# The 512-column weight-stationary product in every stage of a fused encoder layer, with its evictions, gelu and first LayerNorm reordered

## The chip, the cores and the metric

One core of a Trainium2 chip runs the whole layer as one program. The metric is device microseconds of that core, lower is better. Besides the timed runs there is one execution under the hardware profiler, from which all rows of this document are taken.

## The reference

One post-norm layer over 256 tokens of width 2048, all in float32 (cut):

```python
proj = x @ w_in                       # q, k, v (8 heads x 128), u (1024), two gates (2048 each)
g_att, g_ssm = sigmoid(g_att + b), sigmoid(g_ssm + b)
y_att = neighbourhood_attention(q, k, v, rpb) @ w_na_out
y_s = s5_scan(u, forward) + s5_scan(u, backward) + s5_d * u     # 64 groups, 64 complex states
y_s = gelu(y_s); y_s = y_s * sigmoid(y_s @ w_glu + b_glu)
mix = (g_att * y_att + g_ssm * (y_s @ w_s5_out)) @ w_out
h = layer_norm(ALPHA * x + mix)
out = layer_norm(ALPHA * h + (silu(h @ w_ffn_gate) * (h @ w_ffn_up)) @ w_ffn_down)
```

## The kernel before

All weights come as one stream of 464 pieces of 128 x 1024 numbers, in the order in which they are used: 16 for u (pieces 0 to 15, "the U stage"), 16 for v, 12 for each of the 8 heads (q, k and the two gates, two pieces for each of six outputs), 8 + 8 + 8 for the first half of the attention projection (NA1), the GLU and the second half (NA2), 16 for the S5 output (S5O), 32 for the output projection (WO), 176 for gate and up of the feed-forward stage (FF) and 88 for down (DN).

Each piece goes through the same steps. SP's queue loads it into one of 4 raw buffers (`load`). ScalarE rounds it into a high part (`split_hi`, L510), VectorE subtracts to get the low part (`split_lo`, L885); there are 3 buffers for each, so ScalarE may split piece c once TensorE has used piece c-3. TensorE then multiplies high by high, high by low and low by high. The activations are split in the same way: `act16[:, k, 0, :]` is the high part of 256 tokens, `act16[:, k, 1, :]` the low one, side by side. A piece holds 8 weight tiles of 128 x 128.

There are three forms of the product. `prod_a` (L1375) keeps the weight tile in TensorE and issues three matmuls of 256 columns into one half of a bank; u, the heads and the four mixer projections use it. `prod_w` (L1388), used by FF alone, issues one matmul of 512 columns (high weights by both parts, into both halves of the bank) and one of 256; the two halves are added when the bank is emptied. `prod_b` (L1402) keeps the activations in TensorE and streams 512 weight columns; v, WO and DN use it.

What every engine does besides is written out by hand as a list of small steps between the pieces: `if j == 5: ...` behind piece j of head f. Each engine works its own list in order, and semaphores tie them. The steps that matter here:

In a head, TensorE does `turn_b` (four transposes of the next head's S5 matrices; TURN_B says behind which pieces), `s5_in`, `scores`, `s5_out`, `transposes`, `blocks` and `attend`. ScalarE empties the banks (`loop_copy` L663), keeps the turned matrices (`keep_wb` L576, four times), forms exp and the normalised weights. VectorE runs the scans (`scan`, `turn_back`), the softmax maximum, `form_c` (L1022) for the next head and `finish`. POOL computes tables and `form_b` (L438) for the next head. The lag products are stored to memory and loaded again as tb by ScalarE's queue (`stage_tb` L595).

At the end of the heads ScalarE does `loop_copy(HEADS - 1, 5)` and then its list for NA1: the splits, sigmoids of the gates, and behind the fourth split one gelu over all of u and the high part of it. `na_gate` (L1178), `glu_act` and `s5o_evac` (L1218) multiply straight out of the banks.

The banks of WO are (3 + n - N_WO) % 8 (L243). Behind WO VectorE splits three FF pieces, adds the residual (`residual` L1237), takes the moments and normalises h (L1288). TensorE transposes h in 8 groups; ScalarE applies gain and bias to each from the bank (L818) and rounds it (L821), VectorE forms the low part (L889). When all 8 are transposed, POOL multiplies h by the gain and adds the bias in place, in four operations of 2048 columns (L490, L492); the second LayerNorm needs that.

## Time and profile before

| | us |
|---|---|
| timed runs | 1478.47, 1487.91, 1488.67 |
| median | 1487.91 |
| profiled execution | 1480.08 |
| its span, first to last instruction | 1478.3 |

A timeline row has the start in us from the start of the span, the duration, engine, line, operation, what it writes and reads, a count, and in brackets the idle time of the engine ahead of it with what ended it. A matmul's duration is longer than its share of a stream, since matmuls overlap; the pace is the distance between starts. PE is TensorE, PEld its weight loads, DVE VectorE, ACT ScalarE, POOL GpSimd.

### The profile page before, as it was taken

The numbers are of one execution on the slowest core, as the hardware profiler recorded it, in microseconds if no ns is written. First come the engines' busy times: TensorE is split into PE (matmuls) and PEld (weight loads), VectorE is DVE, ScalarE is ACT, GpSimd is POOL, SyncE is SP. The second block draws the span as 40 slices with busy tenths as digits, with TensorE's granted clock in tenths as the row PEclk, the third lists the DMA queues.
The fourth block names the chain that finished last, engine by engine and source line by source line (L and its number), as shares of the span: only waits on it lengthen the run. The fifth ranks groups of instructions, "written<-read, shape, count | busy, mean of one in ns | idle before, by whom it ended". The sixth has DMA issues, their size and how long they took to land.

```text
span 1478.3 us, 25543 instructions
## 1 busy us (share of the span) xinstructions
PE 1406.1 (95%) x10144; PEld 1266.9 (86%) x10144; DVE 931.0 (63%) x1119; ACT 711.2 (48%) x984; POOL 206.0 (14%) x170
## 2 busy tenths in 40 slices
PE   7899999999999899999599999999999999999994
PEld 7789999999999899888488888888888888888883
DVE  7869777887766456665865555555555554545545
ACT  4354555555553664434455445445445444334342
POOL 2784223442310000000500000000000000000002
PEclk9999999999999999999799999999999999999997
DMA  8564545454445467556155555555755555555662
GB/s 286 165 210 159 174 147 169 151 161 153 158 149 166 130 200 274 169 185 200 54 185 186 196 187 186 194 187 185 250 190 185 192 191 192 192 194 192 196 191 80
DMA packets 87700, 266.53 MB, mean 180 GB/s; under 512 B 13760, under 2 KB 22080, under 8 KB 87104
## 3 DMA queue, kind: packets, MB, share of 16 engines
q1 hardware_dynamic: 79472, 259.86, 53.3%
q10 hardware_dynamic: 8144, 5.48, 1.3%
q8 instruction: 62, 1.02, 0.3%
q14 instruction: 22, 0.18, 0.0%
HBM read 260.19 MB, written 5.11 MB: 179 GB/s over the span
## 4 chain that ended last, share of the span: by engine, by line
PE 91%; DVE 6%; ACT 1%; issue 1%; DMA 0%; ACTq 0%; SPq 0%; DVEq 0%
PE bank L1397 22%; PE bank L1398 11%; PE bank L1383 9%; PE bank L1385 9%; PE bank L1384 9%; PE bank L1410 8%; PE bank L1411 8%; PE bank L1412 8%; PE bank L1471 2%; DVE wlo L885 2%; PE bank L1440 1%; DVE act L889 1%; PE bank L1492 1%; PE bank L1518 1%; PE bank L1453 1%
## 5 line engine op out<-in xcount | busy, mean ns | idle before, releaser
L885 DVE TENSOR_TENSOR wlo<-raw,whi 128x1024 fp32r<-128x1024 f32 x464 | 585.9, 1266 | 436.0 <-ACT whi L510 432.9
L510 ACT ACTIVATE whi<-raw 128x1024 fp32r<-128x1024 f32 x464 | 489.7, 1057 | 438.0 <-PE bank L1412 223.0
L1397 PE MATMUL bank<-act,whi 128*128 128x512 f32 x1408 | 491.2, 395 | 10.8 <-DVE wlo L885 10.8
L1398 PE MATMUL bank<-act,wlo 128*128 128x256 f32 x1408 | 391.2, 278 | 0.0
L1397 PEld LDWEIGHTS bank<-act,whi 128*128 128x128 f32 x1408 | 265.1, 188 | 73.0 <-issue 9.9
L1383 PE MATMUL bank<-act,whi 128*128 128x256 f32 x896 | 261.9, 292 | 10.1 <-DVE wlo L885 10.0
L1398 PEld LDWEIGHTS bank<-act,wlo 128*128 128x128 f32 x1408 | 265.6, 189 | 0.0
L1384 PE MATMUL bank<-act,whi 128*128 128x256 f32 x896 | 254.7, 284 | 0.0
L1385 PE MATMUL bank<-act,wlo 128*128 128x256 f32 x896 | 254.6, 284 | 0.0
L1383 PEld LDWEIGHTS bank<-act,whi 128*128 128x128 f32 x896 | 173.0, 193 | 11.3 <-DVE wlo L885 10.7
L1384 PEld LDWEIGHTS bank<-act,whi 128*128 128x128 f32 x896 | 173.0, 193 | 0.5
L1385 PEld LDWEIGHTS bank<-act,wlo 128*128 128x128 f32 x896 | 172.8, 193 | 0.0
L1412 PE MATMUL bank<-whi,mid 128*128 128x512 f32 x352 | 137.0, 389 | 0.0
L1410 PE MATMUL bank<-whi,mid 128*128 128x512 f32 x352 | 137.0, 389 | 0.0
L1411 PE MATMUL bank<-wlo,mid 128*128 128x512 f32 x352 | 137.0, 389 | 0.0
L498 POOL TENSOR_TENSOR hp<-hp,lnrow 128x512 f32<-128x512 f32 x3 | 5.0, 1664 | 724.3 <-ACT hp L877 724.3
L1410 PE MATMUL bank<-whi,act 128*128 128x512 f32 x192 | 76.5, 398 | 7.7 <-DVE wlo L885 4.9
L1410 PEld LDWEIGHTS bank<-whi,mid 128*128 128x128 f32 x352 | 66.1, 188 | 13.8
L1412 PEld LDWEIGHTS bank<-whi,mid 128*128 128x128 f32 x352 | 66.1, 188 | 13.8
L1411 PEld LDWEIGHTS bank<-wlo,mid 128*128 128x128 f32 x352 | 66.1, 188 | 13.5
L1412 PE MATMUL bank<-whi,act 128*128 128x512 f32 x192 | 75.6, 394 | 0.0
L1411 PE MATMUL bank<-wlo,act 128*128 128x512 f32 x192 | 75.5, 393 | 0.0
(162 smaller groups left out, 1600.6 us busy)
## 6 DMA issues: line engine op xcount, KB each, us to landing
raw<-wstream SPq DMA_DIRECT2D x464, 512.0 KB, 4.0
lnrow<-lnrows SPq DMA_DIRECT2D x4, 1024.0 KB, 7.9
xraw<-xT SPq DMA_DIRECT2D x8, 256.0 KB, 5.7
bcn<-bc_rows SPq DMA_DIRECT2D x8, 256.0 KB, 3.0
bm<-bias SPq DMA_DIRECT2D x8, 256.0 KB, 4.1
tb<-lag_dram ACTq DMA_DIRECT2D x32, 64.0 KB, 3.4
hp<-xtok SPq DMA_DIRECT2D x4, 512.0 KB, 4.7
out<-hp SPq DMA_DIRECT2D x8, 256.0 KB, 2.5
```

The source lines that it names most:

```text
L510: act.activation(whi[:, c % SPL, :], raw[:, c % RAW, :], ACT.Copy).then_inc(hi_ready, 1)
L885: dve.tensor_tensor(wlo[:, c % SPL, :], raw[:, c % RAW, :], whi[:, c % SPL, :].bitcast(F32), ALU.subtract).then_inc(lo_ready, 1)
L889: dve.tensor_tensor(o, full, hi.bitcast(F32), ALU.subtract).then_inc(s, 1)
L1383: pe.matmul(bank[:, 0:T], hi, act[:, k0 + i, 0, :], start=start and i == 0, stop=False)
L1384: pe.matmul(bank[:, 0:T], hi, act[:, k0 + i, 1, :], start=False, stop=False)
L1385: mm = pe.matmul(bank[:, 0:T], lo, act[:, k0 + i, 0, :], start=False, stop=stop and i == kn - 1)
L1397: pe.matmul(bank[:, :], hi, both, start=start and i == 0, stop=stop and i == kn - 1)
L1398: mm = pe.matmul(bank[:, 0:T], lo, act16[:, k0 + i, 0, :], start=False, stop=stop and i == kn - 1, skip_group_check=True)
L1410: pe.matmul(banks[t][:, :], a, hi, start=start and i == 0, stop=False)
L1411: pe.matmul(banks[t][:, :], a, lo, start=False, stop=False)
L1412: mm = pe.matmul(banks[t][:, :], b, hi, start=False, stop=stop and i == 1)
L1471: mm = pe.matmul(ps[VB + d][:, o:o + NB], wb[:, r, 4 * d + q, :], ut, start=True, stop=True)
```

## The change

`prod_a` goes; u, the heads and the mixer projections use `prod_w`, which now takes the activations as an argument. So each of their banks holds two halves, and emptying it takes two steps: ScalarE copies the upper half (`cross_in`, `loop_copy`, `cross`), and VectorE adds the lower one (`loop_add`, `add_cross`). In the projections the sum lies in a ring of four buffers xsum, and the multiplication by the gate (`na_mult`) or ScalarE's sigmoid (`glu_act`) comes a piece later from there.

In the heads the second turn of b moves from behind piece 3 to behind piece 4, the scores from 4 to 5, the transposes from 8 to 9, softmax steps one piece later, form_c from (6, 8) to (5, 7), spread_c from 10 to 8, keep_wb to (5, 7, 8, 10). stage_tb goes to SP's queue, ahead of load 7 of each head. The last parameter steps (`powers`) are cut into four.

gelu comes in two halves, behind the second split of NA1, its high parts behind the third and fourth, and the sigmoids of the gates behind those. WO takes banks 5, 6, 4, 7, 0, 1, 2, 3.

Behind WO only two splits stand ahead of the residual; the third comes behind the normalising. VectorE applies gain and bias to every other group of hT. POOL's scaling is cut into 16 operations of 512 columns, each of which waits for a further unit of the feed-forward stage.

```diff
-TURN_B = (2, 3, 5, 7)
+TURN_B = (2, 4, 5, 7)
+KEEP_WB = (5, 7, 8, 10)
...
-                return (3 + n - N_WO) % 8
+                return (5, 6, 4, 7, 0, 1, 2, 3)[n - N_WO]
...
-            for t in range(TT):
-                pool.tensor_tensor(hp[:, t, :], hp[:, t, :], lnrow[:, 0, :], ALU.mult).then_inc(h_step, 1)
-                pool.wait_ge(h_step, 2 * t + 1)
-                pool.tensor_tensor(hp[:, t, :], hp[:, t, :], lnrow[:, 1, :], ALU.add).then_inc(h_step, 1)
+            for n in range(8):
+                v, b = hp[:, n // 4, n % 4 * 512:n % 4 * 512 + 512], slice(n % 4 * 512, n % 4 * 512 + 512)
+                pool.wait_ge(mid_ready, 2 * n + 2)
+                pool.tensor_tensor(v, v, lnrow[:, 0, b], ALU.mult).then_inc(h_step, 1)
+                pool.wait_ge(mid_ready, 2 * n + 3)
+                pool.wait_ge(h_step, 2 * n + 1)
+                pool.tensor_tensor(v, v, lnrow[:, 1, b], ALU.add).then_inc(h_step, 1)
...
+            def cross_in(t, c):
+
+                act.wait_ge(w_used, c + 1)
+                act.activation(u[:, t, :], ps[bank_of(N_U + t)][:, T:2 * T], ACT.Copy).then_inc(in_cross, 1)
...
                 act.wait_ge(w_used, PER_F * f + (H_LOOP + 2 * o + 2))
-                src = ps[bank_of(N_LOOP + o)][:, 0:T]
...
-                act.activation(dst, src, ACT.Copy).then_inc(loop_copied, 1)
+                act.activation(loop_home(f, o), ps[bank_of(N_LOOP + o)][:, T:2 * T], ACT.Copy).then_inc(loop_cross, 1)
...
+            def loop_add(f, o):
+
+                v = loop_home(f, o)
+                dve.wait_ge(loop_cross, 6 * f + o + 1)
+                dve.tensor_tensor(v, ps[bank_of(N_LOOP + o)][:, 0:T], v, ALU.add).then_inc(loop_copied, 1)
...
-                elif j in (14, 15):
+                elif j in (14, 15, 16, 17):
                     powers(j - 14)
...
-            for c in range(3):
+            for c in range(2):
                 split_lo(0, H_FF + c)
...
+            split_lo(0, H_FF + 2)
             for g in range(8):
+                if g % 2 == 0:
+                    dve.wait_ge(hT_psum, g + 2)
+                    if g > 0:
+                        dve.wait_ge(hT_lo, g)
+                    for e in range(2):
+                        t = 2 * g + 2 + e
+                        dve.tensor_scalar(hT[:, 1, e, :], ps[4 + (g + 1) % 4][:, e * T:(e + 1) * T], col[:, 40 + t:41 + t],
+                                          col[:, 56 + t:57 + t], ALU.mult, ALU.add).then_inc(hT_odd, 1)
...
-                    pe.matmul(bank[:, 0:T], hi, act[:, k0 + i, 0, :], start=start and i == 0, stop=False)
-                    pe.matmul(bank[:, 0:T], hi, act[:, k0 + i, 1, :], start=False, stop=False)
-                    mm = pe.matmul(bank[:, 0:T], lo, act[:, k0 + i, 0, :], start=False, stop=stop and i == kn - 1)
...
+                    both = act[:, k0 + i, :, :].rearrange("p h n -> p (h n)")
                     pe.matmul(bank[:, :], hi, both, start=start and i == 0, stop=stop and i == kn - 1)
+                    mm = pe.matmul(bank[:, 0:T], lo, act[:, k0 + i, 0, :], start=False, stop=stop and i == kn - 1,
```

VectorE in the middle of a head (head 1), from the split of piece 4 on. Before (wlo is the low part of a weight piece, mt from bcn and lp is form_c, S is the scores' softmax):

```order
L885 TENSOR_TENSOR wlo<-raw,whi 128x1024
L1125 TENSOR_TENSOR mt<-sb,ef 128x512
L1126 TENSOR_TENSOR mt<-sb,ef 128x512
L1128 TENSOR_TENSOR sb<-mt 128x512
L885 TENSOR_TENSOR wlo<-raw,whi 128x1024 x2
L1035 TENSOR_TENSOR mt<-bcn,lp 128x512
L1036 TENSOR_TENSOR mt<-bcn,lp 128x512
L1038 TENSOR_TENSOR mt<-mt 128x512
L885 TENSOR_TENSOR wlo<-raw,whi 128x1024
L1141 SCALAR_TENSOR_TENSOR S<-bank,bm 128x512
```

The same place of the changed kernel (its lines are numbered anew: L931 is the split, L1209 the addition of `loop_add`):

```order
L931 TENSOR_TENSOR wlo<-raw,whi 128x1024
L1174 TENSOR_TENSOR mt<-sb,ef 128x512
L1175 TENSOR_TENSOR mt<-sb,ef 128x512
L1177 TENSOR_TENSOR sb<-mt 128x512
L1209 TENSOR_TENSOR qk<-bank,qk 128x256
L931 TENSOR_TENSOR wlo<-raw,whi 128x1024
L1084 TENSOR_TENSOR mt<-bcn,lp 128x512
L1085 TENSOR_TENSOR mt<-bcn,lp 128x512
L1087 TENSOR_TENSOR mt<-mt 128x512
L931 TENSOR_TENSOR wlo<-raw,whi 128x1024
L1209 TENSOR_TENSOR qk<-bank,qk 128x256
L931 TENSOR_TENSOR wlo<-raw,whi 128x1024
```

form_c stands ahead of the split of piece 6 where it stood behind it, and the addition that completes k, which the scores need, behind both.

ScalarE at the seam from the last head to the mixer projections, from the transposed weights (PT) on. Before:

```order
L657 ACTIVATE PT<-bank 128x512
L674 ACTIVATE gs<-bank 128x256
L510 ACTIVATE whi<-raw 128x1024
L661 ACTIVATE act8a<-bank 128x256
L731 ACT_TABLE_LOAD
L731 ACTIVATE ga<-ga,col 128x256 x2
L510 ACTIVATE whi<-raw 128x1024
L731 ACTIVATE ga<-ga,col 128x256 x2
L510 ACTIVATE whi<-raw 128x1024
L731 ACTIVATE ga<-ga,col 128x256 x2
L510 ACTIVATE whi<-raw 128x1024
L725 ACT_TABLE_LOAD
```

Now:

```order
L674 ACTIVATE PT<-bank 128x512
L530 ACTIVATE whi<-raw 128x1024
L678 ACTIVATE act8a<-bank 128x256
L685 ACTIVATE gs<-bank 128x256
L530 ACTIVATE whi<-raw 128x1024
L749 ACT_TABLE_LOAD
L749 ACTIVATE u<-u 128x1024 x2
L530 ACTIVATE whi<-raw 128x1024
L685 ACTIVATE gs<-bank 128x256
L755 ACTIVATE act8b<-u 128x4x256
L530 ACTIVATE whi<-raw 128x1024
L755 ACTIVATE act8b<-u 128x4x256
```

The split (whi) comes ahead of the bank copies (gs), and gelu (u from u) ahead of the sigmoids of the gates.

VectorE behind the output projection, from the moments on. Before:

```order
L1263 SCALAR_TENSOR_TENSOR lnm<-lnm 128x2
L1288 TENSOR_SCALAR hp<-hp,lnm 128x512 x8
L889 TENSOR_TENSOR act_52<-hT,act_52 128x2x256 x6
L885 TENSOR_TENSOR wlo<-raw,whi 128x1024
L889 TENSOR_TENSOR act_52<-hT,act_52 128x2x256 x2
```

Now:

```order
L1342 SCALAR_TENSOR_TENSOR lnm<-lnm 128x2
L1367 TENSOR_SCALAR hp<-hp,lnm 128x512 x8
L931 TENSOR_TENSOR wlo<-raw,whi 128x1024
L1376 TENSOR_SCALAR hT<-bank,col 128x256 x2
L935 TENSOR_TENSOR act_52<-hT,act_52 128x2x256 x2
L1376 TENSOR_SCALAR hT<-bank,col 128x256 x2
```

One split and the first two hT operations stand ahead of the first low part of h.

## Rows read from the trace of the kernel before

**Rows 1.** The page: its head, and the shares of the chain.

```profile
span 1478.3 us, 25543 instructions
...
PE 91%; DVE 6%; ACT 1%; issue 1%; DMA 0%; ACTq 0%; SPq 0%; DVEq 0%
```

**Rows 2.** Timeline of TensorE, start us, us, what: two stretches without other work.

```profile
303.10 0.28 PE L1383 MATMUL bank<-act,whi 128*128 128x256 f32 x1
...
307.77 0.28 PE L1383 MATMUL bank<-act,whi 128*128 128x256 f32 x1
...
849.76 0.39 PE L1397 MATMUL bank<-act,whi 128*128 128x512 f32 x1
...
856.69 0.39 PE L1397 MATMUL bank<-act,whi 128*128 128x512 f32 x1
```

**Rows 3.** Waits (us in total, times, longest); then stretches: length, busy times, PEclk, DMA.

```profile
PE bank L1440 <- ACT wb L581: 8.7, 7, 2.4
...
109.98:487.00 377.02, 368.31 (x4279) 359.29 (x4279) 276.51 (x315) 198.49 (x310) 112.04 (x78) 1.00 0.49 158
302.20:349.37 47.17, 46.12 (x543) 45.02 (x541) 35.98 (x41) 26.18 (x41) 17.38 (x12) 1.00 0.51 160
```

**Rows 4.** Timelines of VectorE and TensorE at the end of the U stage.

```profile
50.49 1.27 DVE L885 TENSOR_TENSOR wlo<-raw,whi 128x1024 fp32r<-128x1024 f32 x1
...
63.28 3.26 DVE L885 TENSOR_TENSOR wlo<-raw,whi 128x1024 fp32r<-128x1024 f32 x2
...
64.64 0.77 PE L1410 MATMUL bank<-whi,act 128*128 128x512 f32 x1 [4.87 <-DVE wlo L885]
65.20 0.63 PE L1411 MATMUL bank<-wlo,act 128*128 128x512 f32 x1
```

**Rows 5.** Timelines of TensorE, ScalarE and VectorE from the last head to WO.

```profile
487.99 0.28 PE L1385 MATMUL bank<-act,wlo 128*128 128x256 f32 x1
...
496.86 1.28 ACT L725 ACT_TABLE_LOAD   x1
...
505.22 1.22 DVE L885 TENSOR_TENSOR wlo<-raw,whi 128x1024 fp32r<-128x1024 f32 x1 [6.78 <-ACT whi L510]
...
582.72 1.23 DVE L885 TENSOR_TENSOR wlo<-raw,whi 128x1024 fp32r<-128x1024 f32 x1 [0.52 <-ACT whi L510]
...
616.00 0.50 PE L1410 MATMUL bank<-whi,act 128*128 128x512 f32 x1 [2.80 <-DVE gs L1222]
```

**Rows 6.** Timelines of four engines round the first LayerNorm.

```profile
702.97 0.39 PE L1412 MATMUL bank<-whi,act 128*128 128x512 f32 x1
...
705.68 0.68 DVE L1241 SCALAR_TENSOR_TENSOR hp<-hp,bank 128x512 f32<-128x512 f32 x1
...
719.86 4.63 POOL L490 TENSOR_TENSOR hp<-hp,lnrow 128x2048 f32<-128x2048 f32 x1 [302.53 <-PE bank L1605]
...
719.88 10.09 DVE L889 TENSOR_TENSOR act<-hT,act 128x512 fp32r<-128x512 f32 x2 [0.88 <-ACT act L821]
...
761.97 1.06 ACT L510 ACTIVATE whi<-raw 128x1024 fp32r<-128x1024 f32 x1 [1.20 <-PE bank L1398]
```

**Rows 7.** Timelines of VectorE and POOL within a head (head 4).

```profile
309.08 0.41 DVE L889 TENSOR_TENSOR act8a<-bank,act8a 128x256 fp32r<-128x256 f32 x1
309.41 0.68 DVE L1125 TENSOR_TENSOR mt<-sb,ef 128x512 f32<-128x512 f32 x1
...
319.49 1.22 DVE L885 TENSOR_TENSOR wlo<-raw,whi 128x1024 fp32r<-128x1024 f32 x1
...
322.31 1.23 DVE L1035 TENSOR_TENSOR mt<-bcn,lp 128x512 f32<-128x512 f32 x1
...
326.50 2.31 DVE L885 TENSOR_TENSOR wlo<-raw,whi 128x1024 fp32r<-128x1024 f32 x1
...
319.72 1.59 POOL L477 TENSOR_TENSOR ef<-pt 128x256 f32<-128x256 f32 x1 [5.34 <-DVE sb L1128]
...
323.13 1.37 POOL L451 TENSOR_TENSOR pt<-bcn,kp 128x512 f32<-128x512 f32 x1
```

More of the change, by code:

```diff
@@ L270, in taken, with loop_home @@
             return res_added, 8 + n - N_DN + 1
+        def loop_home(f, o):
+            if o < 2:
+                return qk[:, f % 2, o, :]
+            return (ga if o < 4 else gs)[:, 2 * f + o % 2, :]
         @block.sync
@@ L302, in stage_v, with stage_tb @@
                              ).then_inc(v_staged[f % 2], 16)
+            def stage_tb(f):
+                sp.wait_ge(lags_stored, 16 * f + 16)
+                if f > 0:
+                    sp.wait_ge(y_done, 2 * f - 1)
+                for j in range(Q):
+                    o = 32 * (Q - 1 - j)
+                    sp.dma_start(tb[32 * j:32 * j + 32, :, :, :].rearrange("p q j n -> p q (j n)"),
+                                 lag_dram[:, o:o + P].rearrange("(q r) m -> r q m", r=32)).then_inc(tb_staged, 16)
             for i in range(XP):
@@ L354, in _ @@
                     load(m, c)
[L355 removed]
+            sp.wait_ge(h_step, 16)
             for r in range(2):
@@ L1000, in powers @@
                     stt(li[:, 1, :], lr[:, 0, :], 2.0, li[:, 0, :], ALU.mult, ALU.mult)
+                elif part == 1:
                     a, b = prods(2)
@@ L1006, in powers @@
                     tt(li[:, 2:4, :], b[:, 0], b[:, 1], ALU.add)
-                else:
+                elif part == 2:
                     a, b = prods(3)
@@ L1373, in wait_split, with prod_w @@
                 pe.wait_ge(lo_ready, 12 * m + (c + 1))
-            def prod_a(m, c, act, k0, kn, bank, start, stop, ready=None):
+            def prod_w(m, c, act, k0, kn, bank, start, stop, ready=None):
                 s = c % SPL
@@ L1382, in prod_a @@
                     hi, lo = (w[:, s, i * P:(i + 1) * P] for w in (whi, wlo))
-                    pe.matmul(bank[:, 0:T], hi, act[:, k0 + i, 0, :], start=start and i == 0, stop=False)
-                    pe.matmul(bank[:, 0:T], hi, act[:, k0 + i, 1, :], start=False, stop=False)
-                    mm = pe.matmul(bank[:, 0:T], lo, act[:, k0 + i, 0, :], start=False, stop=stop and i == kn - 1)
-                mm.then_inc(w_used, 1)
-            def prod_w(m, c, k0, kn, bank, start, stop, ready=None):
-                s = c % SPL
-                for i in range(kn):
-                    if ready:
-                        ready(k0 + i)
-                    hi, lo = (w[:, s, i * P:(i + 1) * P] for w in (whi, wlo))
-                    both = act16[:, k0 + i, :, :].rearrange("p h n -> p (h n)")
+                    both = act[:, k0 + i, :, :].rearrange("p h n -> p (h n)")
                     pe.matmul(bank[:, :], hi, both, start=start and i == 0, stop=stop and i == kn - 1)
-                    mm = pe.matmul(bank[:, 0:T], lo, act16[:, k0 + i, 0, :], start=False, stop=stop and i == kn - 1,
+                    mm = pe.matmul(bank[:, 0:T], lo, act[:, k0 + i, 0, :], start=False, stop=stop and i == kn - 1,
                                    skip_group_check=True)
```

237 lines of the change are left out of this document (141 added, 96 removed).

## The prediction

> **What bounds the kernel now.** I read the page first: a span of 1478.3 us, and 91% of the chain that ended last lies on TensorE [rows 1]. So the kernel is bound by TensorE's own pace, plus the places where TensorE is kept waiting. The second view is TensorE's timeline, for the pace. In the three-matmul form 13 weight tiles, 39 matmuls of 256 columns, go from 303.10 to 307.77: 0.359 us a tile, 0.12 between starts. In the form that the feed-forward stage uses, one 512-column matmul and one of 256, 20 tiles go from 849.76 to 856.69: 0.3465 us each [rows 2]. Both stream 768 columns per tile at the full clock; the second issues one matmul and one weight load fewer. Per piece (8 tiles) I take 2.88 and 2.77 us. The output and down projections (512 columns, activations stationary) aren't changed.
>
> The third view is who waited. TensorE waits for ScalarE's copy of wb ahead of the second turn of b, seven times, 8.7 us in all, the longest 2.4 (head 0) [rows 3]: 1.05 us in each of the other six, 1.2 with the restart. At the end of the U stage VectorE is the bound: TensorE waits 4.87 us for a split and then works at the half clock (1.2 of 2.4 GHz: 0.63 us for a matmul that takes 0.39 otherwise) [rows 2, 4]. Between the last head and the output projection 128.0 us pass, from 487.99 to 616.00 [rows 5], where 40 pieces at 2.88 are 115.2. Round the first LayerNorm, 58.9 us pass from 703.2 (end of the matmul of 702.97) to about 762.0, when ScalarE's wait for the eleventh feed-forward piece ends [rows 6]; eleven pieces are 30.5.
>
> **Part 1, the 512-column form.** It reaches 152 pieces: 16 of u, 96 of the heads, 40 of the mixer projections. Saving: 0.107 us each, where TensorE is the bound, so not for u (part 2). That is 10.3 us in the heads and 4.3 in the projections. Added are one VectorE addition from PSUM (0.33 us from start to start; the nearest row is the 128x256 one at 309.08, followed by 309.41 [rows 7]) and, in the projections, one ScalarE copy of the same size per bank.
>
> The Trainium skill, "TensorE: Matmul & The Clock Gate", section "Back-to-back issue gap", gives N/2.4 + 2.5 ns for a lone stream at full clock; as an estimate by it, one matmul fewer is worth 2.5 ns a tile, 2.7 us over 136 pieces in place of 14.6. The rows show 120 ns for 256 columns where the page would have 109, so the trace disagrees, and I go by the rows. The page's other rule (section "The mechanism": a weight load overlaps running matmuls only where the row groups differ) would expose every load; the trace disagrees with that too, since starts 0.12 apart leave no room for one.
>
> **Part 2, the end of the U stage.** VectorE is the bound there, so its work counts. Before, from the split at 50.49 it did the parameter steps and two more splits, and the split of piece 16 began only at 63.28 [rows 4]. Now the last steps lie behind pieces 14, 15, 16 and 17. With the same durations: split 15 ends at 54.2, 16 at 58.2, 17 at 61.3, then the kp steps (3.9) and split 18 at 67.2. TensorE then starts piece 18 at 67.2. Before it was 72.2 (64.64, a piece of 4.8 in the half clock, one of 2.72). So up to 5.0 us; three gaps of 1.1, 1.0 and 2.9 us may still bring the half clock on, which costs about 2 (4.8 against 2.72). Taken: 4.2, bounds 1 and 5. POOL's chain starts 2.4 us later; ScalarE asks for its first result at piece 24, seven pieces on, so that is covered (2.4 us at most without the cover).
>
> **Part 3, the heads.** A head lasts 47.17 us [rows 3]. The second turn moves from behind piece 3 to behind piece 4, one piece (2.77) later, so its 1.2 us wait goes in heads 1 to 6. What is late next is VectorE. It runs without a pause from piece 2 to piece 5, now with two more additions (0.7 us), and form_c comes one piece earlier. ScalarE's copy of the last gs bank no longer stands ahead of split 2, so this run starts 1.8 us earlier: split 5 begins at 318.4 where it was 319.49, and form_c at 319.6. POOL's ef and, 3.4 us later, form_b follow the end of the turn back (319.72 before, 318.2 now), and beside them form_c takes 4.2 us and a split 2.31 instead of 1.22 [rows 7]. I take one contended op of form_c, since form_b now starts 1.9 us after it: form_c to 322.3, split 6 to 324.5, then the addition to k at 324.9 to 325.3. The scores need it, and TensorE is there at 324.5. So a new wait of 0.6 us, bounds 0 and 2.3 (form_c fully contended). Queued behind it on TensorE are the first s5_out, a turn and piece 6. Heads 1 to 6: 1.28 + 1.2 - 0.6 = 1.9 each, 11.3 in all. Head 7 has neither: 1.3. In head 0 VectorE starts its run late (the v copies), the old wait of 2.4 us becomes about 1.6 before piece 4 and 1.9 before the scores: 0. Sum 12.6, bounds 0 and 15. The tb loads on SP's queue instead of ScalarE's (4 issues a head, ahead of load 7) wait for lags kept some 4 us before, and land 10 us before their use; nothing. spread_c two pieces earlier makes ScalarE wait for form_c (about 3 us), ahead of split 9, which leaves 1 us of VectorE's lead: nothing, if form_c is not later than above.
>
> **Part 4, mixer projections.** Before, ScalarE waited for the last head's last piece, to copy its bank, ahead of the first projection's split; then came three table loads (1.28 each), and gelu and the copy behind it over all 2048 columns in one block, which made VectorE wait 6.78 us [rows 5]. Now the split comes first, gelu comes in halves two pieces earlier, and one load goes. Laid out from those durations, splits 2 to 5 of this stage are ready 1.2 to 1.8 us ahead of TensorE. The additions of the last three banks lie within the next loop, and the output projection starts in banks 5 and 6, which nobody has to empty, where it waited 2.80 for gs [rows 5]. VectorE's pitch in the S5 output rises from 2.36 (it idled 0.52 of 2.88 [rows 5]) by one addition, 0.41 and the wait between, to at most 2.80 per piece of 2.77; its lead of 3 us covers that for 16 pieces. So 128.0 becomes 40 x 2.77 + 0.4 = 111.3: 16.7 us, bounds 9 and 17.
>
> **Part 5, LayerNorm 1 and the scaling.** POOL's four 2048-column operations start at 719.86, and beside them two of VectorE's low parts take 10.09 us [rows 6]; TensorE loses some 11 us. They become 16 of 512 columns, each released by a later feed-forward unit. Also the third split no longer stands ahead of the residual (it begins at 705.68, and could at 703.3 [rows 6]: 2.3 us), and VectorE forms every other hT, so that a pair takes about 2.1 us instead of 3.1. But split 2 and two hT operations now stand ahead of the first low part: it ends at 713.6 (before: 714.3). Then piece 0 ends at 718.0 and the eleventh at 718.0 + 10 x 2.77 = 745.7: 16.2 us. The half clock may fall on piece 0, so 15.5, bounds 9 and 18. The 16 POOL pieces (some 1.2 to 1.7 us each) can hold a split up by one of them; the 3 us of lead cover it.
>
> **Sum.** 4.2 + 12.6 + 16.7 + 15.5 = 49.0 us off the profiled execution's own 1480.08 (span 1478.3 and 1.8 around it): 1431. That execution lies 7.8 below the median of the runs shown (1487.91), which reach from 1478.47 to 1488.67, so the median after may lie anywhere from 1431 to 1440; I say 1435.
>
> **Rivals.**
> A: the heads become VectorE's. form_c fully contended, scores wait 2.3 us in six heads and 4 in head 0: 12 us lost, 1447. For it: rows 7 show the contention. Against: it begins with POOL's form_b, not with ef.
> B: the shorter form saves nothing here, because the 13 ns a tile by which the two paces differ belong to the feed-forward stage and not to the form: 14.6 lost, 1450. Against: both paces are measured [rows 2]. By the Trainium skill's 2.5 ns (above) most of that would be lost too.
> C: the scaling is only moved. If each of the 16 POOL pieces stops VectorE long enough to stop TensorE, 1.2 us each, 19 come back: 1454. For: two-input VectorE work stands still beside POOL [rows 6]. Against: the lead.
> D: slower. The scores wait 2.3 us in each head and the clock halves behind it, as it did at 64.64 behind a wait of 4.87; at 0.63 us for 0.39 a stretch of 10 us costs up to 5. That is 7.3 a head, and from 6.2 a head on (49 over 8) the whole gain is gone: with 7.3, 58 back, 1493. Against: the waits of 1.2 and 2.4 us left the clock at 1.00 throughout the heads [rows 3].
>
> **How the numbers follow.** Forecast 0.64, A 0.16, B 0.04, C 0.08, D 0.03, and 0.05 for mixtures in the stages of parts 2, 4 and 5 that end near 1460. The forecast's own range is 1420 to 1445; with A and most of C the range is 1420 to 1457. About 1% is what a measurement of this kernel can tell from no change; faster by more than that (below 1473) holds in all but D and a rest: 0.95, within 1% 0.03, slower 0.02.
>
> **What would show it.** Right: starts 0.23 and 0.12 us apart in the heads; no wait before the turns and one under 1 us before the scores; about 111 us from last head to output projection; about 43 us from the end of the output projection to the eleventh feed-forward piece, with POOL rows of 512 columns spread behind it; feed-forward pieces still 2.77 apart. Wrong: heads above 46 us, a wait for VectorE in the feed-forward stage, or more than 0.35 us a tile.

## The result, and the profile after

The changed kernel takes 1462.15 us (median of 4 runs, 1459.49 to 1463.29), the kernel before 1488.17 beside it: a ratio of 0.983, 95% interval 0.981 to 0.985. The forecast was 1435 with a range of 1420 to 1457. The direction was right, the size wrong: 26 us came of the 53 between 1488 and the forecast. The profiled executions are 1480.08 and 1463.29, 16.8 apart where the sum said 49.0.

Stage by stage, from the starts of TensorE's first matmul of each stage in the two traces (a piece's start is every 16th or 24th matmul of its form; e3 is the experiment below):

| stage | before | after | e3 | predicted change | measured change |
|---|---|---|---|---|---|
| to the first piece of head 0 | 115.26 | 111.41 | 111.24 | -4.2 | -3.85 |
| head 0 | 48.49 | 53.91 | 47.23 | 0 | +5.42 |
| heads 1 to 6, each | 47.17 | 48.93, 47.37, 47.31, 48.93, 47.37, 45.03 | 45.03 | -1.9 | +1.8 to -2.1 |
| head 7 | 44.34 | 40.68 | 40.68 | with the next two | -3.66 |
| NA1, GLU, NA2 | 27.87, 23.04, 24.89 | 22.61, 22.61, 22.62 | as after | heads 7 and projections -18.0 | |
| S5 output | 49.11 | 45.22 | 45.22 | | |
| output projection to 13th feed-forward piece | 148.48 | 135.14 | 134.97 | -15.5 | -13.34 |
| from there to the down projection (164 pieces) | 454.83 | 463.58 | 463.58 | 0 | +8.75 |
| down projection, to its last piece | 236.67 | 236.65 | 236.65 | 0 | 0 |

The page of the kernel after, its head and the shares of the chain, answers to [rows 1]. VectorE, 6% of the chain before, has 13%:

```profile
span 1461.5 us, 23307 instructions
...
PE 85%; DVE 13%; ACT 1%; issue 0%; DMA 0%; ACTq 0%; SPq 0%; DVEq 0%
```

The waits of the kernel after (us in total, times, longest) answer to the first of [rows 3]. TensorE's wait for wb ahead of the turns is no longer in the list; in its place stands one ahead of the scores, for the addition that completes k:

```profile
PE bank L1577 <- DVE qk L1209: 13.8, 6, 3.6
```

Heads 0, 1, 2 and 6 of the kernel after, as stretches (length, busy times of PE, PEld, DVE, ACT, POOL, PEclk, DMA share, GB/s), answer to the rest of [rows 3]. The granted clock is not 1.00 in the first two, and where no next head's matrices are formed (the last) VectorE works 5 us less and the head is 2.3 shorter:

```profile
111.41:165.31 53.90, 48.56 (x445) 41.81 (x444) 43.95 (x51) 25.81 (x40) 17.14 (x12) 0.94 0.50 149
165.31:214.24 48.93, 46.90 (x446) 40.72 (x445) 39.14 (x47) 26.44 (x41) 16.83 (x12) 0.97 0.52 154
214.24:261.61 47.37, 45.34 (x447) 39.59 (x445) 39.05 (x46) 26.31 (x41) 16.86 (x12) 1.00 0.54 158
...
405.21:450.24 45.03, 45.03 (x446) 39.57 (x445) 33.82 (x47) 26.31 (x41) 6.71 (x6) 1.00 0.52 158
```

VectorE, POOL and TensorE in head 4 of the kernel after answer to [rows 7] (start, us, what, idle time ahead). The split of piece 5 begins beside POOL's ef and takes 1.71 instead of 1.2; form_c's three operations (L1084, L1085, L1087) run beside form_b, and the split behind them takes 2.29. From the start of the first split to the end of the addition to k are 8.4 us; the prediction had 6.9:

```profile
322.16 1.71 DVE L931 TENSOR_TENSOR wlo<-raw,whi 128x1024 fp32r<-128x1024 f32 x1
323.80 1.23 DVE L1084 TENSOR_TENSOR mt<-bcn,lp 128x512 f32<-128x512 f32 x1
324.95 1.59 DVE L1085 TENSOR_TENSOR mt<-bcn,lp 128x512 f32<-128x512 f32 x1
326.57 1.48 DVE L1087 TENSOR_TENSOR mt<-mt 128x512 f32<-128x512 f32 x1
327.98 2.29 DVE L931 TENSOR_TENSOR wlo<-raw,whi 128x1024 fp32r<-128x1024 f32 x1
330.20 0.41 DVE L1209 TENSOR_TENSOR qk<-bank,qk 128x256 f32<-128x256 f32 x1
...
322.06 0.74 POOL L494 TENSOR_TENSOR ef<-pt 128x256 f32<-128x256 f32 x1 [5.34 <-DVE sb L1177]
322.75 1.72 POOL L495 TENSOR_TENSOR ef<-pt 128x256 f32<-128x256 f32 x1
324.61 1.38 POOL L468 TENSOR_TENSOR pt<-bcn,kp 128x512 f32<-128x512 f32 x1
...
330.67 2.08 PE L1577 MATMUL bank<-qk 128*128 128x256 f32 x4 [2.03 <-DVE qk L1209]
```

The pace, read as in [rows 2]: 22 tiles from the first to the last of these rows, 0.3536 us each, where the same, unchanged code had 0.3465 before:

```profile
849.36 0.40 PE L1472 MATMUL bank<-act,whi 128*128 128x512 f32 x1
...
857.14 0.40 PE L1472 MATMUL bank<-act,whi 128*128 128x512 f32 x1
```

At the first LayerNorm TensorE waits once for the normalised rows and once for the rounding of hT; the scaling's pieces lie far apart behind that, and the output projection has no wait in its first row, which answers to the last of [rows 5]:

```profile
603.98 0.40 PE L1485 MATMUL bank<-whi,act 128*128 128x512 f32 x1
...
696.32 3.37 PE L1680 MATMUL bank<-ident,hp 128*128 128x128 f32 x16 [5.08 <-DVE hp L1367]
701.85 0.63 PE L1680 MATMUL bank<-ident,hp 128*128 128x128 f32 x4 [2.16 <-ACT act L867]
...
729.49 2.27 POOL L509 TENSOR_TENSOR hp<-hp,lnrow 128x512 f32<-128x512 f32 x1 [308.72 <-DVE ev L1407]
740.70 2.36 POOL L512 TENSOR_TENSOR hp<-hp,lnrow 128x512 f32<-128x512 f32 x1 [8.93 <-DVE ev L1407]
```

So two things are missing from the 49.0: the heads, 18.6 us off the forecast (5.4 of them in head 0), and the pace of the 512-column form, everywhere.

### The profile page after: what moved, and what is told of

Read it like the earlier page. It is cut to its first block, busy times and chain, and to the rows that moved or that the text cites. A ratio compares the mean times of both kernels' runs of the same rounds, so it can differ in the third digit from the quotient of the medians.

```text
span 1461.5 us, 23307 instructions
## 1 busy us (share of the span) xinstructions
PE 1407.5 (96%) x8928; PEld 1204.8 (82%) x8928; DVE 958.6 (66%) x1216; ACT 721.5 (49%) x1025; POOL 221.1 (15%) x182
## 4 chain that ended last, share of the span: by engine, by line
PE 85%; DVE 13%; ACT 1%; issue 0%; DMA 0%; ACTq 0%; SPq 0%; DVEq 0%
PE bank L1472 36%; PE bank L1473 18%; PE bank L1485 8%; PE bank L1487 8%; PE bank L1486 8%; DVE wlo L931 4%; PE bank L1546 1%; PE bank L1567 1%; PE bank L1515 1%; PE bank L1577 1%; DVE sb L1166 1%; DVE sb L1177 1%; DVE mt L1085 1%; DVE mt L1087 1%; PE bank L1593 1%; PE bank L1528 1%
## 5 line engine op out<-in xcount | busy, mean ns | idle before, releaser
L931 DVE TENSOR_TENSOR wlo<-raw,whi 128x1024 fp32r<-128x1024 f32 x464 | 588.1, 1269 | 391.5 <-ACT whi L530 387.8
L1472 PE MATMUL bank<-act,whi 128*128 128x512 f32 x2304 | 824.0, 402 | 10.7 <-DVE wlo L931 10.6
L1472 PEld LDWEIGHTS bank<-act,whi 128*128 128x128 f32 x2304 | 434.5, 189 | 116.7 <-DVE wlo L931 10.5
L518 POOL TENSOR_TENSOR hp<-hp,lnrow 128x512 f32<-128x512 f32 x3 | 5.0, 1665 | 546.2 <-ACT hp L923 546.2
L509 POOL TENSOR_TENSOR hp<-hp,lnrow 128x512 f32<-128x512 f32 x8 | 18.8, 2352 | 371.3 <-DVE ev L1407 371.3
L1472 PE MATMUL bank<-act8b,whi 128*128 128x512 f32 x192 | 67.9, 399 | 0.0
L489 POOL TENSOR_TENSOR pt<-base 128x256 f32<-128x256 f32 x32 | 33.7, 1080 | 162.5 <-ACT bp L547 162.5
L834 ACT ACTIVATE gsum<-bank 128x256 f32<-128x256 f32 x44 | 16.9, 383 | 76.4 <-PE bank L1473 76.4
L841 ACT ACTIVATE usum<-bank 128x256 f32<-128x256 f32 x44 | 16.9, 383 | 75.6 <-PE bank L1473 75.6
L1473 PE MATMUL bank<-act8b,wlo 128*128 128x256 f32 x192 | 53.9, 281 | 0.0
```

Of the source, the lines that this page charges most:

```text
L489: pool.tensor_tensor(t[i], a, b, ALU.mult).then_inc(tab_prod, 1)
L509: pool.tensor_tensor(v, v, lnrow[:, 0, b], ALU.mult).then_inc(h_step, 1)
L834: act.activation(gsum[:, b, :], ps[bank_of(N_FF + 2 * i)][:, T:2 * T], ACT.Copy).then_inc(g_cross, 1)
L841: act.activation(usum[:, b, :], ps[bank_of(N_FF + (2 * i + 1) % 6)][:, T:2 * T], ACT.Copy).then_inc(u_cross, 1)
L931: dve.tensor_tensor(wlo[:, c % SPL, :], raw[:, c % RAW, :], whi[:, c % SPL, :].bitcast(F32), ALU.subtract).then_inc(lo_ready, 1)
L1472: pe.matmul(bank[:, :], hi, both, start=start and i == 0, stop=stop and i == kn - 1)
```

## The experiments

Each was timed beside the kernel before, whose medians were 1487.36, 1488.09 and 1487.66 in the three rounds (e1 to e4, e5 to e8, e9 to e12). e3, e4 and e6 change the kernel after; e5, e7, e8, e10, e11 and e12 change e3 and are compared with it, and e9 changes e8.

**e1_before_again**: the kernel before, no edit.

> The kernel before, unchanged. Before's own runs lie at 1478.5 to 1480 and at 1488; its profiled execution (1480.08) has feed-forward pieces of 2.773 us (0.3466 a tile). Theory S (the pace of the 512-column form is a property of the execution: one of two levels, 2.773 or 2.827 a piece): the runs fall on 1479 or 1488 again, and the profiled one, if it is near 1488, has 164 feed-forward pieces of 2.827, 8.9 us more, and nothing else longer. Theory K (the pace is a property of the kernel's code and buffers): 2.773 in every profile of this kernel; the 9 us between its runs then come from elsewhere (half clock, for one).

Measured: 1487.67 (1480.23 to 1491.86), and 1487.77 for the profiled execution, 7.7 more than the 1480.08 the prediction was made from. Its 164 feed-forward pieces from the 13th on, as a stretch (columns as above):

```profile
763.39:1226.96 463.57, 463.57 (x2626) 402.08 (x2625) 266.78 (x328) 226.66 (x328) 0.00 (x0) 1.00 0.56 190
```

The same 164 pieces in the first profile of the kernel before:

```profile
764.48:1219.31 454.83, 454.83 (x2627) 397.65 (x2625) 266.85 (x328) 226.47 (x328) 0.00 (x0) 1.00 0.58 194
```

TensorE has no idle time in either, the clock is 1.00 in both, and one is 8.74 longer: 2.827 against 2.773 a piece. Theory S holds, theory K falls. With 0.4 for the pieces ahead of these the pace is 9.1 us between the two executions; the start up to the heads was 1.45 shorter in e1 (113.81 against 115.26), which leaves the 7.7. The second profile has both paces in one execution. Its feed-forward piece 1 starts at 718.74 and piece 2 at 721.51, 2.77 apart; then TensorE waits 9.62 us beside POOL's scaling, and behind that the 13th and 14th pieces are 2.83 apart:

```profile
718.74 0.39 PE L1397 MATMUL bank<-act,whi 128*128 128x512 f32 x1
...
721.51 0.39 PE L1397 MATMUL bank<-act,whi 128*128 128x512 f32 x1
...
734.07 0.76 PE L1397 MATMUL bank<-act,whi 128*128 128x512 f32 x1 [9.62 <-DVE wlo L885]
...
763.39 0.40 PE L1397 MATMUL bank<-act,whi 128*128 128x512 f32 x1
...
766.22 0.40 PE L1397 MATMUL bank<-act,whi 128*128 128x512 f32 x1
```

So here a pace is taken up behind a pause and kept over all the pieces that follow. The starts show it as a pattern: at the fast pace the tiles take 0.344 and 0.350 in turn, at the slow one 0.350, 0.361 and 0.349. In all the timed runs of the kernel before, 46 of them, 9 lie at 1478 to 1480, 6 at 1483 to 1484 and 31 at 1487 to 1493. By these levels the fast pace of 1480.08 was a rare one; of the 46 runs only the one at 1487.77 was profiled, so that the other low ones had the same pace is inferred. What makes the group in between isn't known.

**e2_after_again**: the changed kernel, no edit.

> The changed kernel, unchanged. Theory S: if the profiled execution is of the fast level, the feed-forward pieces take 2.773 and it ends near 1447, 16 us earlier (300 pieces by 0.054); otherwise near 1462 again. Theory K: 2.827 a piece and 1460 to 1463 in every run.

Measured: 1459.86 (1459.48 to 1461.74). The profiled execution (1459.98) has 463.57 us for the 164 pieces, 2.827 each, as the first. The fast pace appeared in none of 8 runs; the theories are not told apart by this one. It has the wait before the scores in six heads again, and the half clock behind it only in heads 0 and 4, where the first had it in 0, 1 and 4: a head of 48.92 with it and heads of 47.32 to 47.37 without.

**e3_formc_late**: form_c behind the addition to k.

```diff
-                    if f + 1 < KS and j in (5, 7):
-                        form_c(f + 1, j // 2 - 2)
                     if j in (0, 2) and f > 0:
                         loop_add(f - 1, 4 + j // 2)
                     if j in (4, 6, 8, 10):
                         loop_add(f, j // 2 - 2)
+                    if f + 1 < KS and j in (6, 8):
+                        form_c(f + 1, j // 2 - 3)
...
-                        if j == 8:
+                        if j == 10:
                             spread_c(f + 1)
```

> The changed kernel with form_c back behind the splits of pieces 6 and 8 and behind the addition that completes k, and spread_c back at 10. Theory A (the scores wait because form_c, slowed by POOL's form_b, stands ahead of the addition to k): the wait of TensorE ahead of the scores (3.8 us in head 0, 2.2 in the others) falls under 0.6, the half clock behind it goes, and heads 0 to 6 last 45.2 each: 1462 becomes 1444 (head 0: 5 to 7 us, heads 1 to 5: 2.2 each, the half clock 1.6 in two heads). Rival A2 (VectorE has too much work ahead of piece 7 in any order, so the wait moves): TensorE waits for the split of piece 7 or the block matmuls instead, heads stay at 47.4, 1460.

Measured: 1439.63 (1438.93 to 1441.51), 20 us below the changed kernel beside it (e2), 4 below what was expected, and a ratio of 0.968 (0.963 to 0.972) to the kernel before. The stretches are heads 0 and 4:

```profile
111.24:158.47 47.23, 45.53 (x445) 39.59 (x444) 41.66 (x50) 25.82 (x40) 17.74 (x12) 1.00 0.53 163
293.56:338.58 45.02, 45.02 (x446) 39.56 (x445) 37.83 (x46) 26.55 (x41) 17.41 (x12) 1.00 0.54 169
```

TensorE is busy for the whole of head 4 and the clock is 1.00. There is no wait before the scores in any head, though POOL's form_b still runs beside VectorE's work. Theory A holds, A2 falls. By heads, the wait and the clock behind it cost 6.7, 3.9, 2.3, 2.3, 3.9 and 2.3 us: 21.4.

**e4_scaling_whole**: POOL's scaling in four operations again.

```diff
-            for n in range(8):
...
+            for t in range(TT):
+                pool.tensor_tensor(hp[:, t, :], hp[:, t, :], lnrow[:, 0, :], ALU.mult).then_inc(h_step, 4)
+                pool.wait_ge(h_step, 8 * t + 4)
+                pool.tensor_tensor(hp[:, t, :], hp[:, t, :], lnrow[:, 1, :], ALU.add).then_inc(h_step, 4)
```

> The changed kernel with POOL's scaling of h back in four operations of 2048 columns right behind the transposes; hT shared out and the third split late, as changed. If the pieces are what saves time at the first LayerNorm: VectorE's low parts take some 5 us each beside POOL's operations, and 9 to 11 us come back (1472). If the 16 pieces cost something in the feed-forward stage (a pace of 2.827 in place of 2.773 through VectorE or memory traffic): the pace falls back to 2.773 behind the scaling, 8.7 us are gained there, and the time stays at 1462 to 1464.

Measured: runs of 1465.05, 1465.65, 1474.53 and 1476.09. The profiled one (1476.09) has pieces of 2.827, and its second to twelfth feed-forward pieces take 45.46 us where the changed kernel needs 31.09: 14.4. The longest wait behind it:

```profile
712.59 9.08 DVE L932 TENSOR_TENSOR act<-hT,act 128x512 fp32r<-128x512 f32 x2
721.59 5.51 DVE L928 TENSOR_TENSOR wlo<-raw,whi 128x1024 fp32r<-128x1024 f32 x1
...
727.15 0.79 PE L1469 MATMUL bank<-act,whi 128*128 128x512 f32 x1 [12.09 <-DVE wlo L928]
```

So the pieces are what saves time there, and they don't set the pace: it is 2.827 with the scaling over, here and in e1, and e7, e8 and e12 below have the fast pace with POOL's 16 pieces beside it. The heads, which e4 leaves as they are, wait again for 2.02 to 2.04 us in heads 1 to 5, and the half clock follows in heads 1 and 5 (granted clock 0.97) besides head 0. The two runs near 1465 weren't profiled; a fast pace would explain the 9 us, but that is argued only.

**e5_orders**: on e3, the matmuls of a piece in another order.

```diff
+                ORDERS = {"plain": lambda kn: [(i, l) for i in range(kn) for l in (0, 1)],
+                          "snake": lambda kn: [(i, l) for i in range(kn) for l in ((0, 1) if i % 2 == 0 else (1, 0))],
+                          "split": lambda kn: [(i, 0) for i in range(kn)] + [(i, 1) for i in range(kn)],
+                          "pairs": lambda kn: [(i + e, l) for i in range(0, kn, 2) for l in (0, 1) for e in (0, 1)]}
...
+                       last_head if j == 0 else None, form=("snake", "split", "pairs")[j // 8])
...
+                        prod_w(m, H_FF + 4 * i + q, act16, 8 * (q % 2), 8, ps[bank_of(n)], q % 2 == 0, q % 2 == 1,
+                               form='snake')
```

> The kernel of e3_formc_late with the matmuls of a piece issued in another order, the same ones: NA1 high, low, low, high (two neighbouring tiles swap their order); GLU all eight high ones and then all eight low ones; NA2 high, high, low, low; feed-forward as NA1. In e1 and before, the pieces of a stage go at one of two steady paces, 2.773 or 2.827, with spacings that repeat every 2 or every 3 tiles, and a pause can change which. Theory L (TensorE's issue locks into one of several patterns, set by the sequence of matmuls and loads): another order has another pace, somewhere between 2.56 (768 columns at 2.4 GHz, times 8) and 2.90, and if feed-forward comes to 2.773 or less the time is 1431 or less. Rival (the pace depends only on what is streamed and loaded): 2.827 in all four, 1440.

Measured: 1434.06 (1432.11 to 1435.15). A piece takes 2.787 in NA1, 2.791 in GLU, 2.787 in NA2 and, over the 164 feed-forward pieces, 2.787; the S5 output, in the plain order, has 2.827 in the same execution. The edit also leaves the first 12 feed-forward pieces in the plain order, and this gives the cleanest view, the change of order in the middle of a stream. Pieces 11, 12 and 13 (counted from 0) start at:

```profile
711.65 0.40 PE L1481 MATMUL bank<-act,whi 128*128 128x512 f32 x1
...
714.48 0.40 PE L1481 MATMUL bank<-act,whi 128*128 128x512 f32 x1
...
717.27 0.39 PE L1481 MATMUL bank<-act,whi 128*128 128x512 f32 x1
```

The last plain piece takes 2.83, the first in the new order 2.79, with no wait between. The rival falls: the order of the same matmuls sets a pace, and the three orders with neighbours of equal width lie between the two paces of the plain one. That TensorE locks into a pattern, as theory L has it, is a picture of this and not shown.

**e6_formb_waits**: on the changed kernel, POOL's form_b held back.

```diff
                     pool.wait_ge(tab_ready, 2 * f)
+                    pool.wait_ge(c_formed, 2 * f - 1)
```

> The changed kernel (form_c early, as changed) with POOL's form_b held until the first part of form_c is done, so that the two don't run side by side. Theory A by contention: form_c's three operations take 0.7 to 1.25 us each instead of 1.2 to 1.6, and the split behind it 1.2 instead of 2.3; the wait ahead of the scores (2.2 us) falls to 0 to 0.5 in heads 1 to 5, which last 45.0 to 45.5: some 9 us off, 1450. Rival (form_c's place alone makes the wait, whoever is beside it): the wait stays above 1.5 us. A later form_b could make the turn of b wait instead; that would show as a wait of TensorE for wb or bp.

Measured: 1442.01 (1441.06 to 1443.01), 8 below what was expected, heads 1 to 6 of 45.03, head 0 of 48.42 with a wait of 0.86 before the scores. VectorE in head 4, and POOL's form_b behind form_c:

```profile
307.21 1.71 DVE L932 TENSOR_TENSOR wlo<-raw,whi 128x1024 fp32r<-128x1024 f32 x1
308.85 1.23 DVE L1085 TENSOR_TENSOR mt<-bcn,lp 128x512 f32<-128x512 f32 x1
310.00 0.68 DVE L1086 TENSOR_TENSOR mt<-bcn,lp 128x512 f32<-128x512 f32 x1
310.71 0.69 DVE L1088 TENSOR_TENSOR mt<-mt 128x512 f32<-128x512 f32 x1
311.32 1.22 DVE L932 TENSOR_TENSOR wlo<-raw,whi 128x1024 fp32r<-128x1024 f32 x1
312.45 0.42 DVE L1210 TENSOR_TENSOR qk<-bank,qk 128x256 f32<-128x256 f32 x1
...
311.57 1.94 POOL L469 TENSOR_TENSOR pt<-bcn,kp 128x512 f32<-128x512 f32 x1 [2.05 <-DVE mt L1088]
```

5.7 us from the split to the addition's end instead of 8.4, with form_c in its new, early place: the contention makes the wait, and the rival falls. It takes both, the early place and the contention, since e3 removes the wait by the place alone. Beside ef the first split still takes 1.71 and form_c's first operation 1.23, so ef contends too. The Trainium skill, "SBUF — State Buffer", section "SBUF: two separate sides", calls the port pair that VectorE and GpSimd share an exclusive lock, taken by one instruction for its whole length. The rows agree: three operations of 1.23, 0.68 and 0.69 here take 1.23, 1.59 and 1.48 when POOL runs beside them, and the addition, one of whose inputs is a bank, takes 0.41 or 0.42 with form_b beside it in both. The later of two instructions is the one that is held up, which such a lock would give: before, the split began 0.23 us ahead of ef, and it took 1.22 and ef's first operation 1.59 [rows 7]; in the changed kernel ef began 0.10 ahead, and it took 0.74 and the split 1.71.

**e7_turn_early**: on e3, the second turn of b behind piece 3.

```diff
-TURN_B = (2, 4, 5, 7)
-KEEP_WB = (5, 7, 8, 10)
+TURN_B = (2, 3, 5, 7)
+KEEP_WB = (5, 6, 8, 10)
```

> The kernel of e3_formc_late with the second turn of b back behind piece 3 (keep_wb at 5, 6, 8, 10). By part 3 of the prediction TensorE waits 1.2 us for wb in each of heads 1 to 6 and 2 in head 0: heads of 46.1 to 46.2 instead of 45.03, 7 to 9 us more, 1448. Rival (the wait was made by the bank copies and the split order, which changed as well): heads stay at 45.0 and the time at 1440.

Measured: 1440.32 (1432.48 to 1442.79). Heads 1 to 6 stay at 45.02, without a wait, and there the rival holds: the wait before the turn doesn't come back with its old place. In head 0 it does come back, but most of it stands in for shorter waits that head 0 has anyway (1.39 and 0.31 in e3), and the head is only 0.54 longer (47.77 against 47.23):

```profile
127.13 0.41 PE L1515 MATMUL bank<-ident,bp 128*128 128x128 f32 x2 [2.64 <-ACT wb L601]
```

The profiled execution (span 1430.7) has the fast pace in the feed-forward stage, 454.83 for the 164 pieces. The projections ahead of it, in the same execution, have 2.827 a piece.

**e8_ht_scalar**: on e3, ScalarE scales all eight groups of hT.

```diff
-                if g % 2 == 0:
...
+                for e in range(2):
+                    t = 2 * g + e
+                    act.activation(hT[:, g % 2, e, :], ps[4 + g % 4][:, e * T:(e + 1) * T], ACT.Identity,
+                                   scale=col[:, 40 + t:41 + t], bias=col[:, 56 + t:57 + t]).then_inc(hT_f32, 1)
```

> The kernel of e3_formc_late with all eight groups of hT scaled by ScalarE again. By part 5 of the prediction a pair of groups took 3.1 us on ScalarE and takes 2.1 shared: four pairs, 3 to 4 us later for the first feed-forward piece, 1443. Rival (VectorE, which has a split and the residual in that stretch, gains nothing from the sharing): 1440 or below.

Measured: runs of 1430.07, 1430.15, 1438.62 and 1440.56; the profiled execution has the fast pace. From the output projection to the 13th feed-forward piece 132.60 us pass, and 134.97 in e3, of which the fast pace explains 0.6. The stretch up to the first feed-forward piece alone, in which the 512-column form with weights kept doesn't occur, says the same: the piece comes 97.4 us behind that of the output projection (97.3 in e9), and 98.2 to 98.7 in the nine profiled executions that share hT and have the third split late. The rival holds: sharing hT out brings nothing, and seems to cost about 1 us.

**e9_snake_all**: on e8, the order high, low, low, high in every piece.

```diff
-                    pe.matmul(bank[:, :], hi, both, start=start and i == 0, stop=stop and i == kn - 1)
-                    mm = pe.matmul(bank[:, 0:T], lo, act[:, k0 + i, 0, :], start=False, stop=stop and i == kn - 1,
-                                   skip_group_check=True)
+                    for low_part in ((0, 1) if i % 2 == 0 else (1, 0)):
+                        if low_part:
+                            mm = pe.matmul(bank[:, 0:T], wlo[:, s, i * P:(i + 1) * P], act[:, k0 + i, 0, :], start=False,
+                                           stop=stop and i == kn - 1, skip_group_check=True)
+                        else:
+                            mm = pe.matmul(bank[:, :], whi[:, s, i * P:(i + 1) * P], both, start=start and i == 0,
+                                           stop=stop and i == kn - 1, skip_group_check=True)
```

> The kernel of e8_ht_scalar (form_c late, hT by ScalarE alone) with the matmuls of the 512-column form in the order high, low, low, high in all 328 pieces. e5_orders showed 2.787 us a piece for this order in every stage and run, where the plain order has 2.827 or 2.773. Theory L (the order fixes the pattern): all runs near one value, with no second level: 128 pieces of heads and projections 0.04 faster each (5 us), 176 in feed-forward 0.04 faster than the slow level (7 us): from 1440 to 1428 to 1430, and heads of 44.5 us. Rival (a head has other work between its pieces, so no steady pattern forms there and the order changes nothing in heads): heads of 45.0, 1432.

Measured: 1430.31 (six runs, 1429.84 to 1431.32), ratio 0.963 (0.960 to 0.966): the best version here, and its runs show no levels. Six runs are few for that: 15 of the 46 runs of the kernel before lie off its main level, and at that rate six runs alike would come about once in ten by chance. The 164 pieces:

```profile
712.53:1169.55 457.02, 457.02 (x2626) 398.76 (x2625) 266.91 (x328) 226.32 (x328) 35.47 (x15) 1.00 0.59 193
```

The rival holds for heads 1 to 6, which fall only from 45.03 to 44.94; head 7 (40.32) and the projections (2.787 a piece) gain as expected.

**e10_powers_two**: on e3, the last parameter steps in two blocks.

```diff
-                elif j in (14, 15, 16, 17):
-                    powers(j - 14)
+                elif j in (14, 15):
+                    powers(2 * (j - 14))
+                    powers(2 * (j - 14) + 1)
```

> The kernel of e3_formc_late with the last parameter steps again in two blocks, behind pieces 14 and 15. By part 2 of the prediction piece 18 starts some 4 to 5 us later (71 instead of 66.6) and the heads begin 3 to 4.5 us later: 1443. Rival (TensorE lacks work there either way, and the gain seen at the start of the heads came from the shorter form and the two-step evictions): no difference, 1440.

Measured: 1443.29 (1435.81 to 1446.90). Piece 18 starts at 71.16 instead of 66.60 and head 0 at 114.24 instead of 111.24, where it starts at 110.5 to 111.4 in every profile with the steps in four. Part 2 holds.

**e11_split_ahead**: on e3, the third split ahead of the residual.

```diff
-            for c in range(2):
+            for c in range(3):
                 split_lo(0, H_FF + c)
...
-            split_lo(0, H_FF + 2)
             for g in range(8):
```

> The kernel of e3_formc_late with the third feed-forward split back ahead of the residual. By part 5 of the prediction it delays the residual and all behind it by 1.2 to 2.3 us: 1441 to 1442, seen between the output projection's start and the twelfth feed-forward piece (134.97 in e3). Rival (it only moves from one place of VectorE's chain to another): 134.5 to 135.3.

Measured: 1441.93 (1433.30 to 1443.80), 2.3 more than e3. TensorE's wait ahead of the transposes of h grows by 2.3, but the one behind it, for ScalarE's rounding, falls from 1.9 to 0.7. So the first feed-forward piece comes 1.1 later (99.8 us behind the start of the output projection; 98.2 to 98.7 with the split late), and up to the 13th piece 136.47 pass instead of 134.97. The split's place counts, at some 1.1 to 1.5 us of the profile. The first transposes in TensorE's timeline of e3:

```profile
674.72 1.11 PE L1680 MATMUL bank<-ident,hp 128*128 128x128 f32 x4 [5.08 <-DVE hp L1367]
```

And of e11:

```profile
676.90 0.90 PE L1679 MATMUL bank<-ident,hp 128*128 128x128 f32 x3 [7.36 <-DVE hp L1367]
```

**e12_wo_banks**: on e3, the output projection's banks in the old order.

```diff
-                return (5, 6, 4, 7, 0, 1, 2, 3)[n - N_WO]
+                return (3 + n - N_WO) % 8
```

> The kernel of e3_formc_late with the output projection's banks back in the order (3 + n) mod 8. By part 4 of the prediction TensorE then waits for the last additions and gates of the S5 output ahead of the output projection, as the 2.80 us before: 1442 to 1443. Rival (the earlier additions already take that wait away, so that idle banks are worth nothing): under 0.5 us, 1440.

Measured: 1444.61 (1434.69 to 1445.28). The wait is back at its old length, and the S5 output stage lasts 48.18 instead of 45.22; the rival falls. The median is 5.0 above e3's; the other 2 have no place that the profiled execution shows, which had the fast pace.

```profile
584.82 0.51 PE L1485 MATMUL bank<-whi,act 128*128 128x512 f32 x1 [2.80 <-DVE xsum L1241]
```

## Why the prediction was wrong

**Part 1, mis-sized; the step that failed is "Saving: 0.107 us each", resting on "both paces are measured".** They were, but in one execution, and that one was of a rare kind. Three matmuls a tile take 2.880 a piece in both profiles of the kernel before. The 512-column form takes 2.827 in most executions and 2.773 in a few, and those few (before, e7, e8, e12) have it in the feed-forward stage alone. So the saving is 0.053 a piece and not 0.107, or 6.6 ns a tile, between the 13 that the prediction took and the 2.5 that it set beside them: 7.2 us over the 136 pieces. And the feed-forward stage, put at no change, ran 164 pieces at 2.827 against the 2.773 of the profiled execution: 8.75. With 0.6 for its first pieces, the pace makes 16.7 of the 32.2 us missing between the profiled executions. Rival B had the right sum in part (the difference belongs in half to the pace and not to the form) but not the right reason as it stands: the feed-forward stage has either pace, so the stage alone doesn't decide. Whether it has a share is open, since in the plain order the projections showed 2.827 in every profile. The prediction asked how 1480.08 stood to the median of 1487.91 and only carried the 7.8 us over as an uncertainty of the median; by e1 the pace is behind the 7.8, and it changed two terms of the sum.

**Part 3, the heads: rival A, which had 0.16, was right.** The step that failed is "I take one contended op of form_c, since form_b now starts 1.9 us after it". The split ahead of form_c was itself held up by ef (1.71 for 1.2), so form_c began later. And ef, which now started first and was not held up itself (0.74 for 1.59), let form_b begin 2.55 us behind ef's start instead of the 3.4 read from rows 7. The prediction had this order in its own numbers, ef at 318.2 and the split at 318.4, and gave both their old durations. So form_b began only 0.8 us behind form_c; two of form_c's operations and the split behind them ran beside it. "Against: it begins with POOL's form_b, not with ef" is what e6 contradicts. The wait was 2.03 in head 4 and 3.63, the longest, in head 0, close to the rival's 2.3 and 4. Rival A's price still fell short, since part of rival D came with it: the half clock followed the wait in heads 0, 1 and 4 (e2: 0 and 4) at 1.6 us a head, about 3 in head 0 (1.8 in e2), and not the 5 a head that D needed. "The waits of 1.2 and 2.4 us left the clock at 1.00" was true, and no evidence for another place: behind 2.03 us here it fell in two heads of five (one of five in e2, two of five in e4). All told 21.4 us by e3, where the forecast had 3.6 in heads 1 to 6 and a balanced head 0.

The 1.2 us a head for the turn did come, and a little more: heads of 45.03 are 2.14 below before, 0.64 of it by the pace. But moving the turn isn't what brought it, since e7 moves it back and loses nothing in those heads. That this term came true is luck. The copies of banks that went from ScalarE's place ahead of keep_wb remain as the reason; they weren't tried alone.

**Part 2 was right within what can be told**: 3.85 against 4.2, piece 18 at 66.36 against 67.2, and e10 gives 3.0 for the blocks alone. The start of the heads moves by up to 1.45 us between executions of one kernel (115.26 and 113.81 in the two profiles of the kernel before), so against the second of them the gain is 2.4.

**Part 4 was right but for the pace.** NA1 to the output projection went from 124.90 to 113.06, and the 3 us wait ahead of NA1 is gone: 14.8 against 16.7, and the pace, 40 pieces by 0.054, is 2.2 and so covers the 1.9 between. e12 gives the idle banks their 2.8 to 3.0.

**Part 5 was right in sum, partly by luck**: 13.34 against 15.5, 0.6 of the rest by the pace. But its terms were off both ways. e4 gives the scaling's pieces 14.4 in the profile, more than the 11 taken. The loss was that large before, too: the same eleven pieces took 44.24 us there (granted clock 0.88; 0.85 in e4), where they take 30.5 without a wait: 13.7 lost, the half clock included, and not some 11. The late split is worth 1.1 to 1.5 of the 2.3 forecast (e11). The sharing of hT was put at 1 us a pair and is worth nothing or less (e8). Rival C is wrong: with 35 us of POOL's pieces beside them, the 164 feed-forward pieces take 463.58, and 463.57 in e1 with none, and TensorE waits in neither.

Set together: the pace 16.7, the heads' waits 17.8 above those forecast, 1.9 in parts 2 and 5, less 1.8 (heads 1 to 6), 1.9 (head 0) and 0.3 (head 7 and the projections) by which the stages did better than laid out, the pace and the wait apart: 32.4, of 32.2 missing.

What stays open is which pause leads to which pace. It is told here by what ran before and after pauses (in e1 from fast to slow, in e7, e8 and e12 from 2.827 in the projections to 2.773 behind the output projection and the LayerNorm), and not by a cause.

## What to carry to other kernels

Where runs of one kernel lie in levels (here 1478, 1483 and 1488), profile it more than once before a sum is made from one pace, and ask what the same unchanged code does in each. Work put on VectorE ahead of something that TensorE waits for has to be sized with all of POOL's operations beside it, the one before it included, for the whole length of the run of work and not operation by operation. And of two steps in one list, the short one that another engine waits for goes first: form_c one piece later, behind that short step, gave 20 us of 1460 (e3 against e2).

## What the runs showed of the hardware

The same instructions in the same order ran at 2.773 or 2.827 us a piece, with the clock at 1.00 and no idle time, over 164 pieces without a change (2.773 in before, e7, e8 and e12; 2.827 in e1, after, e2, e3, e4, e6, e10 and e11). The pace was seen to change across a pause. Issuing the same matmuls so that neighbours have equal widths gave 2.787 to 2.791 in all the stages looked at in e5 and e9, and in e9 six timed runs within 1.5 us, where the five of e7 and the four of e8, in the plain order, spread over 10.

Two-input VectorE operations of 128x512 took 0.68 us alone and 1.2 to 1.8 beside POOL's, and one of 128x1024 1.2 alone and up to 2.3; an addition with one input in a bank stayed at 0.41. Behind equal waits of 2.03 us of TensorE, in the same place of successive heads, the granted clock fell in five of fifteen (after, e2, e4).
